# Expert matmuls in plain fp32 on column tiles of the array: sample tokens on two tiles of 64 columns, prompt tokens on four tiles of 32

## The reference

```python
gate, idx = lax.top_k(jnp.swapaxes(aff, 1, 2), cap)
xe = x[bidx, idx]
hid = jax.nn.silu(jnp.einsum('becd,edf->becf', xe, w_gate)) * jnp.einsum('becd,edf->becf', xe, w_up)
ye = jnp.einsum('becf,efd->becd', hid, w_down) * gate[..., None].astype(x.dtype)
return jnp.zeros_like(x).at[bidx, idx].add(ye)
```

## Time and profile before

| | |
|---|---|
| median of 3 runs | 1448.78 us (1447.79 to 1450.2) |
| span of the profiled execution | 1445.4 us |
| time beside that span | the page lists none; the median lies 3.4 us above the span |
| PE busy | 1339.9 us (93%) |
| PEld (weight loads of PE) busy | 965.0 us (67%) |
| DVE busy | 993.1 us (69%) |
| ACT busy | 836.3 us (58%) |
| POOL busy | 445.4 us (31%) |
| DMA | 339.25 MB, mean 235 GB/s |

### The profile page before, as it was taken

How to read it: one execution, slowest core, us unless ns; L and a number is a source line. 1 busy time by engine, 2 the same in 40 slices (tenths; PEclk the granted TensorE clock), 3 DMA queues, 4 the chain that set the end, 5 groups by cost and what they waited for, 6 DMA issues and landing times. The chain is left out here.

```text
span 1445.4 us, 19018 instructions
## 1 busy us (share of the span) xinstructions
PE 1339.9 (93%) x7225; PEld 965.0 (67%) x7225; DVE 993.1 (69%) x1410; ACT 836.3 (58%) x1217; POOL 445.4 (31%) x271
## 2 busy tenths in 40 slices
PE   5999999889998999999999999999898799999995
PEld 1756567766786666666668997555687566666663
DVE  1536515677647888888877628666656788888876
ACT  2623114666324777777765468555423677777773
POOL 0001105585002144444420041465202134444431
PEclk8999999999998999999999999999999999999998
DMA  9688760221526999999973120050243799999965
GB/s 364 239 323 334 298 219 13 79 97 45 192 118 234 381 378 381 387 385 384 385 246 86 33 62 35 2 218 1 96 185 158 289 388 383 383 380 386 384 258 182
DMA packets 64146, 339.25 MB, mean 235 GB/s; under 512 B 17188, under 2 KB 23032, under 8 KB 45624
## 3 DMA queue, kind: packets, MB, share of 16 engines
q1 hardware_dynamic: 57432, 315.29, 56.4%
q0 software_dynamic: 6048, 20.65, 5.9%
q10 hardware_dynamic: 576, 2.10, 0.4%
HBM read 314.12 MB, written 23.89 MB: 234 GB/s over the span
## 5 line engine op out<-in xcount | busy, mean ns | idle before, releaser
L1859 POOL TENSOR_TENSOR modrow<-modrow,proj 80x1024 f32<-80x1024 f32 x30 | 132.1, 4404 | 312.5 <-ACT modrow L1979 312.5
L2011 DVE TENSOR_TENSOR wlow<-wraw,proj_rounded 128x2048 fp32r<-128x2048 f32 x96 | 217.0, 2287 | 5.7 <-ACT proj_rounded L1953 5.7
L1888 PE MATMUL psum<-wlow,proj_rounded 128*80 128x512 f32 x512 | 203.0, 397 | 0.0
L1953 ACT ACTIVATE proj_rounded<-wraw 128x2048 fp32r<-128x2048 f32 x96 | 179.8, 1907 | 16.5 <-PEq L1432 16.5
L1887 PE MATMUL psum<-proj_rounded 128*80 128x512 f32 x376 | 150.9, 401 | 2.1 <-DVE proj_rounded L2016 2.1
L1889 PE MATMUL psum<-proj_rounded 128*80 128x512 f32 x376 | 147.9, 393 | 0.0
L1888 PEld LDWEIGHTS psum<-wlow,proj_rounded 128*80 128x80 f32 x512 | 76.9, 150 | 40.0 <-issue 1.6
L1336 POOL TENSOR_SCALAR ring<-ring,small 128x640 f32<-128x640 f32 x48 | 90.3, 1885 | 41.5 <-DVE small L1275 40.8
L2011 DVE TENSOR_TENSOR wlow<-wraw,xr_rounded 128x2048 fp32r<-128x2048 f32 x32 | 73.3, 2291 | 42.3 <-ACT xr_rounded L1953 42.3
L1888 PE MATMUL psum<-wlow,small_rounded 128*80 128x512 f32 x256 | 100.8, 394 | 0.0
L1266 DVE TENSOR_REDUCE small<-psum 128x1 f32<-128x640 f32 (+1 forms) x80 | 57.3, 716 | 55.1 <-PE psum L1241 54.4
(11 more groups left out here) (537 smaller groups left out, 3347.6 us busy)
## 6 DMA issues: line engine op xcount, KB each, us to landing
wraw<-in_exp_w_gate_dram SPq DMA_DIRECT2D x32, 2048.0 KB, 23.8
wraw<-in_exp_w_up_dram SPq DMA_DIRECT2D x32, 2048.0 KB, 24.3
wraw<-in_exp_w_down_dram SPq DMA_DIRECT2D x32, 2048.0 KB, 23.7
ring<-in_ada_w_dram SPq DMA_DIRECT2D x29, 1024.0 KB, 6.8
hold<-in_ada_w_dram SPq DMA_DIRECT2D x14, 1024.0 KB, 6.5
ring<-in_ev_w_in_dram SPq DMA_DIRECT2D x4, 2048.0 KB, 12.2
xr<-x_rows SPq DMA_DIRECT2D x15, 512.0 KB, 6.9
proj<-in_ada_w_dram SPq DMA_DIRECT2D x5, 1024.0 KB, 9.2
```

The lines of the kernel that those rows point to most:

```text
L1859: pool.tensor_tensor(ye[0:CAP, :], ye[0:CAP, :], g2[0:CAP, :], ALU.mult).then_inc(s["ye"], 1)
L1888: pe.matmul(dst, xs[:, 0, k, :], wl, start=False, stop=False)
L1953: act.activation(high_of(m, h), raw_of(m, h), ACT.Copy).then_inc(s["high"], 1)
L2011: dve.tensor_tensor(low_of(m, h), raw_of(m, h), high_of(m, h), ALU.subtract).then_inc(s["low"], 1)
```

## The change

Only `experts` changes. TensorE reads the raw float32 weights and raw float32 tokens, so nothing is split there: `weights_high`, `weights_low`, `product` and the second copies of the turned rows are gone.

The array is used in tiles of columns. `samples` issues two matmuls with 64 stationary columns (the sample tokens) and 512 moving columns each; one writes partitions 0 to 63, the other 64 to 127. For gate and up the two tiles hold one of the matrices each, for down the two halves of its columns. `prompts` issues four matmuls with 16 stationary columns (the prompt tokens) and 256 moving columns, on the tiles at partitions 0, 32, 64 and 96. The two kinds stand in blocks of four steps of the contraction: four times `samples`, then four times `prompts`.

`into_hidden(e, h)` now works on gate(e) and up(e) together and waits for both loads. `mm` rises by two after its second half. On PE, `turn(e+1)` stands between the two halves. The copies out of the transposes are single (ACT one half of the rows, DVE the other), with two buffers for the turned rows. The scaling by gate and g2 is on DVE for every expert, six instructions each (`weigh_sample` twice, `weigh_prompt` four times); POOL only issues the indirect DMAs. g2 and the gates are laid out by tiles, with six small loads and six small copies at the start of the block.

```diff
--- before.py
+++ after.py
...
@@ -1853,11 +1841,7 @@
                                                 bass.IndirectOffsetOnAxis(ap=idx[:, e:e + 1], axis=0)).then_inc(s[f"gat{e % 2}"], 16)
 
                     def scatter(e):
-                        pool.wait_ge(s["ys"], 2 * (e + 1))
-                        if e == 0:
-                            pool.wait_ge(s["g2"], 32)
-                        pool.tensor_tensor(ye[0:CAP, :], ye[0:CAP, :], g2[0:CAP, :], ALU.mult).then_inc(s["ye"], 1)
-                        pool.wait_ge(s["ye"], e + 1)
+                        pool.wait_ge(s["ys"], e + 1)
                         pool.indirect_dma_start(x_rows, bass.IndirectOffsetOnAxis(ap=idx[:, e:e + 1], axis=0), ye[0:CAP, :], None,
                                                 compute_op=ALU.add).then_inc(s["sc"], 16)
 
...
-                    def product(dst, xs, m, k, h, at, first, last):
-
-                        wh, wl = high_of(m, h)[:, at:at + 512], low_of(m, h)[:, at:at + 512]
-                        pe.matmul(dst, xs[:, 0, k, :], wh, start=first, stop=False)
-                        pe.matmul(dst, xs[:, 0, k, :], wl, start=False, stop=False)
-                        return pe.matmul(dst, xs[:, 1, k, :], wh, start=False, stop=last)
-
-                    def into_hidden(e, n):
-                        m = PLACE_OF[n, e]
-                        if n == 0:
-                            pe.wait_ge(s["xL"], 2 * e + 2)
+                    def samples(b, xs, pair, first, last):
+
+                        for c in range(2):
+                            pe.matmul(psum[c * CAPS:(c + 1) * CAPS, b, :], xs[:, 0:CAPS], pair[c], start=first, stop=last)
+
+                    def prompts(b, xs, pair, first, last):
+
+                        for q in range(4):
+                            mm = pe.matmul(psum[quad(q, CAPP), b, 0:QP], xs[:, CAPS:CAP], pair[q // 2][:, q % 2 * QP:(q % 2 + 1) * QP],
+                                           start=first, stop=last)
+                        return mm
+
+                    def into_hidden(e, h):
+                        gate_at, up_at = PLACE_OF[0, e], PLACE_OF[1, e]
+                        if h == 0:
+                            pe.wait_ge(s["xca"], e + 1)
+                            pe.wait_ge(s["xcd"], e + 1)
                             if e:
-                                pe.wait_ge(s["hs"], e)
-                        elif e:
-                            pe.wait_ge(s["hid"], e)
-                        for h in range(2):
-                            pe.wait_ge(s["low"], 2 * m + h + 1)
-                            for k in range(4 * h, 4 * h + 4):
-                                mm = product(bank(2 + n)[0:CAP, :], xgT, m, k, h, (k % 4) * 512, k == 0, k == KD - 1)
-                            if h == 0:
-                                mm.then_inc(s["half"], 1)
-                        mm.then_inc(s["mm"], 1)
+                                pe.wait_ge(s["hid"], e)
+                            for m in (gate_at, up_at):
+                                pe.wait_ge(ready[m % NSLOT], 16 * (m // NSLOT + 1))
+                        pairs = [[wraw[m % NSLOT][:, k * 512:(k + 1) * 512] for m in (gate_at, up_at)] for k in range(KD)]
+                        for k in range(4 * h, 4 * h + 4):
+                            samples(2, xgT[:, e % 2, k, :], pairs[k], k == 0, k == KD - 1)
+                        for k in range(4 * h, 4 * h + 4):
+                            mm = prompts(4, xgT[:, e % 2, k, :], pairs[k], k == 0, k == KD - 1)
+                        if h:
+                            mm.then_inc(s["mm"], 2)
 
...
                     def down(e):
                         m = PLACE_OF[2, e]
-                        pe.wait_ge(s["hL"], e + 1)
+                        pe.wait_ge(s["hc"], e + 1)
                         if e:
-                            pe.wait_ge(s["ys"], 2 * e)
-                        for h in range(2):
-                            pe.wait_ge(s["low"], 2 * m + h + 1)
-                            for f in range(2 * h, 2 * h + 2):
-                                for c in range(2):
-                                    mm = product(bank(4 + c)[0:CAP, :], hidT, m, f, h, (f % 2) * D + c * 512, f == 0, f == FB - 1)
-                            if h == 0:
-                                mm.then_inc(s["half"], 1)
+                            pe.wait_ge(s["ys"], e)
+                        pe.wait_ge(ready[m % NSLOT], 16 * (m // NSLOT + 1))
+                        pairs = [[wraw[m % NSLOT][:, f * D + c * 512:f * D + (c + 1) * 512] for c in range(2)] for f in range(FB)]
+                        for f in range(FB):
+                            samples(5, hidT[:, f, :], pairs[f], f == 0, f == FB - 1)
+                        for f in range(FB):
+                            mm = prompts(3, hidT[:, f, :], pairs[f], f == 0, f == FB - 1)
                         mm.then_inc(s["mm"], 1)
 
                     keep_busy(pe, 10, 7)
@@ -1932,9 +1922,9 @@
                         into_hidden(e, 0)
                         if e:
                             turn_hidden(e - 1)
-                        into_hidden(e, 1)
                         if e + 1 < NE:
                             turn(e + 1)
+                        into_hidden(e, 1)
                         if e:
                             down(e - 1)
                     turn_hidden(NE - 1)
...
-                    def weights_high(m):
-                        act.wait_ge(ready[m % NSLOT], 16 * (m // NSLOT + 1))
-                        for h in range(2):
-                            if m >= 3:
-                                act.wait_ge(s["mm"] if h else s["half"], m - 2)
-                            act.activation(high_of(m, h), raw_of(m, h), ACT.Copy).then_inc(s["high"], 1)
-
...
+                    def turned_hidden(e):
                         act.wait_ge(s["hT"], e + 1)
                         if e:
                             act.wait_ge(s["mm"], PLACE_OF[2, e - 1] + 1)
-                        act.activation(hidT[:, 0], bank(6)[:, 0:FB * CAP].rearrange("p (k c) -> p k c", k=FB), ACT.Copy).then_inc(s["hH"], 1)
-
-                    def weigh(e):
-                        act.wait_ge(s["mm"], PLACE_OF[2, e] + 1)
+                        act.activation(hidT, bank(6)[:, 0:FB * CAP].rearrange("p (k c) -> p k c", k=FB), ACT.Copy).then_inc(s["hc"], 1)
+
+                    def gate_hidden(e):
+                        act.wait_ge(s["mm"], PLACE_OF[1, e] + 1)
                         if e:
-                            act.wait_ge(s["sc"], 16 * e)
-                        for c in range(2):
-                            act.activation(ye[0:CAP, c * 512:(c + 1) * 512], bank(4 + c)[0:CAP, :], ACT.Copy, scale=gate[:, e:e + 1]).then_inc(s["ys"], 1)
-
-                    weights_high(0)
-                    turn_high(0)
...
-                    def weights_low(m, lo=0, hi=2):
-                        for h in range(lo, hi):
-                            dve.wait_ge(s["high"], 2 * m + h + 1)
-                            dve.tensor_tensor(low_of(m, h), raw_of(m, h), high_of(m, h), ALU.subtract).then_inc(s["low"], 1)
-
...
                     def hidden(e):
-                        dve.wait_ge(s["hs"], e + 1)
-                        dve.wait_ge(s["mm"], PLACE_OF[1, e] + 1)
-                        dve.tensor_tensor(hid[0:CAP, :], hid[0:CAP, :], bank(3)[0:CAP, :], ALU.mult).then_inc(s["hid"], 1)
-
-                    weights_low(0, 0, 1)
-                    turn_low(0)
-                    weights_low(0, 1, 2)
-                    weights_low(1)
+                        if e:
+                            dve.wait_ge(s["hT"], e)
+                        dve.wait_ge(s["hs"], 3 * e + 1)
+                        dve.tensor_tensor(hid[0:CAPS, :], sg[S2, 0:FF], psum[S2, 2, :], ALU.mult)
+                        dve.wait_ge(s["hs"], 3 * e + 3)
+                        for q in range(2):
+                            ins = dve.tensor_tensor(hid[CAPS:CAP, q * QP:(q + 1) * QP], sg[quad(2 + q, CAPP), FF:FF + QP], psum[quad(2 + q, CAPP), 4, 0:QP], ALU.mult)
+                        ins.then_inc(s["hid"], 1)
+
+                    def weigh_sample(e, y, c):
+                        rows = slice(c * CAPS, (c + 1) * CAPS)
+                        return dve.scalar_tensor_tensor(out=y[0:CAPS, c * 512:(c + 1) * 512], in0=psum[rows, 5, :], scalar=gd[rows, 0, e:e + 1], in1=g2s[rows, :],
+                                                        op0=ALU.mult, op1=ALU.mult)
+
+                    def weigh_prompt(e, y, q):
+                        rows = quad(q, CAPP)
+                        return dve.scalar_tensor_tensor(out=y[CAPS:CAP, q * QP:(q + 1) * QP], in0=psum[rows, 3, 0:QP],
+                                                        scalar=gd[rows, 1, e:e + 1], in1=g2p[rows, :], op0=ALU.mult, op1=ALU.mult)
+
+                    def weigh(e):
+                        dve.wait_ge(s["mm"], PLACE_OF[2, e] + 1)
+                        if e:
```

(31 more changed lines are left out.)

98 lines of the change are left out of this document (34 added, 64 removed).

## The result

The changed kernel took 1452.8 us (median of 20 runs), the kernel before 1447.0 us (20 runs). The ratio is 1.0055, with a 95% interval from 1.0041 to 1.0068: slower by about half a per cent. The medians lie 5.8 us apart, the means of the 20 runs 7.9. The profiled execution has a span of 1449.6 us, against 1445.4.

What follows compares the result with a forecast made beforehand. PE and DMA together were taken to bound the expert blocks, at 17.9 and 18.3 us an expert. Terms -15.8 + 0.1 + 2.0 = -13.7 us gave 1431.7 profiled, 1435 us as median; forecast's own range 1427 to 1443.

Steps and rivals of the forecast that it cites:

- The rows give two passes of 0.21 us for 512 plain fp32 columns: TensorE's expert work: profile rows read as two passes per plain fp32 matmul, giving 10.0 us an expert against 17.9.
- A full-width matmul of 512 columns costs 10.46 us over 24, 0.44: Price read from a profile row for one plain fp32 matmul, used to size TensorE's work for an expert.
- The rule that I set aside: Skill's four passes for true FP32: a round 0.86 us, an expert about 17.5 us, no relief for PE.
- this rival: Four passes: PE needs 17.5 us an expert, DMA's 18.3 still hides it; 1439 us in all, chance 0.03.
- Tiles side by side: On TensorE, column tiles work simultaneously in both widths, so four tiles cost what one matmul costs.
- The steady part gains nothing: Experts before the block ends: DMA stays full at 18.3 us an expert, so PE's lighter work saves no time.
- DMA bounds at 18.3 us once TensorE has less to do: Expert blocks: DMA needs 18.3 us for an expert, while PE has 10.0 us of work and waits.
- The end of layer 1 gains: After layer 1's last weight: SP's reload starts 16.9 us earlier, less 1.1 for a cold clock, 15.8 us saved.
- the assumed work: TensorE's forecast work for one expert: 10.0 us with transposes, against 17.9 before.
- Each weight lands when it landed before: Steady part: weight landing times stay unchanged; layer 1's last up lands at 1387.4 us.
- The end of layer 0: Token numbers behind the weights hold this exit: 0.1 us slower, plus 2.0 for odd_front's cold start.
- The low clock binds: Rival: PE stays at 1.2 GHz throughout, 20.0 us an expert against 17.9; 1500 us in all, chance 0.13.

Runs made afterwards that it cites:

- the run with half the rounds: Changed kernel with half of each contraction left out, so two of every four samples and prompts rounds remain; 1436.4 us, ratio 0.9938 against the kernel before.

## Why the prediction was wrong, point by point

- **The step that failed** is "The rows give two passes of 0.21 us for 512 plain fp32 columns", and "A full-width matmul of 512 columns costs 10.46 us over 24, 0.44" ahead of it. I divided by the records of a row as if they were matmuls of the program. L2376 has 12 matmuls in the program, so 0.87 each; in L171's 16 records there are 8 matmuls, two rounds of four tiles and not four, 0.92 each with the change; in L1223's x4 there is one round of two tiles, 0.58. All three rows had the factor of two in them, and they agreed with each other because all three were read in the same wrong way. Counting the matmuls in the listing of the program against the x of the page would have shown it before any run.
- **The rule that I set aside was right.** The Trainium skill (FP8 and Floating Point Precision, section TensorE Precision Notes) says four passes for true FP32. The trace agrees: 0.86 us for 512 columns, two records of 0.43, where one fp32r product starts 0.23 us after another. By it TensorE's expert comes to the 17.5 that the forecast worked out for this rival; measured 17.83, the rest being 0.14 instead of 0.1 for a change and 1.52 us of transposes.
- **The time of that rival, 1439, was wrong too.** It took the last weight's landing as what TensorE waits for at the end. With 17.8 us an expert TensorE never catches up with the loads, and the end of the block is TensorE's own, as before.
- **Tiles side by side**: right, 7 ns apart, in both widths.
- **"The steady part gains nothing"**: right in size (17.83 against 17.89), for another reason. That DMA bounds at 18.3 us once TensorE has less to do: right within 0.2 (18.15 in the run with half the rounds).
- **"The end of layer 1 gains" 15.8 us**: it lost 2.7. With the assumed work, in the trace of the half rounds, the block is 10.2 us shorter where the forecast has 16.9 up to `last_result`, so the direction held and the size was 6.7 us too large. "Each weight lands when it landed before" is 4.9 us of it: the load of up(15) was issued at 1348.33 us and took 41.5 to land, 260.4 us behind the block's first load, and the forecast has 255.5 (1387.4 less 1131.87). The other 1.8 came behind it, where `down(15)` waited 3.03 us for `ys` and then ran at half clock. Why the last load landed later was not tested.
- **The end of layer 0**: +0.1 and +2.0 for the cold start were forecast; +2.5 in the block and +1.7 in the odd layer's front came. The nearness of the 2.0 and the 1.7 is partly luck: the forecast had TensorE rest for about 17 us there, and it rested 2.5. The scalings were sized well (3.3 against 3.6).
- **The wait that I missed**: `down(15)` for `ys`. The forecast prices the six scalings, and doesn't ask who waits for those of expert 14. Its 3.0 us stand in both layers, 2.5 of them on the path in layer 1 alone.
- **"The low clock binds"**: with half the rounds the clock was 0.81 and did not bind.

What stays open: why the clock fell behind the pause of 3.03 us in some executions and not in others, and what share of the difference that is. 0.6 us or so of layer 1's difference and the spread of the odd layer are not assigned.

## What to carry to other kernels

Before a price per operation is taken from a grouped row, set the row's count against the count in the program; an operation that the hardware runs in several instructions shows as several records, and its price is off by that factor. When a pricing row and a written rule differ by exactly two, suspect the count. And where one helper's output is read in more pieces than before, ask at the block's end who waits for the last piece but one: banks that are free there take the wait away, and the order of blocks can hide the pieces.

## What the runs showed of the hardware that was not expected

- A plain fp32 matmul is two records of the trace, each 0.43 us for 512 columns at full clock, at full width and on column tiles alike; for 256 columns on tiles of 32 the records of a tile are 0.216 us apart.
- A change between two column tilings costs TensorE 0.14 us (2.48 us for 18).
- The pause of 3.0 us for `ys` was followed by 1.2 GHz in some executions and not in others; behind the pause of 2.5 us ahead of `last_result` the clock fell in every trace that has it, at once or after some matmuls. The cold start costs the odd layer's front 1.7 to 2.8 us.
- DMA at full share moved 378 to 384 GB/s in this mixture of loads, gathers and scatters, with ACT and DVE busy for 137 and 152 of 179 us or for 21 and 55.
